# Six modulation jobs moved from attention to stand behind feed-forward units

## What is computed

```python
def ada_params(cond, w, b):
    m = (jax.nn.silu(cond) @ w + b)[..., None, :]
    return jnp.split(m, N_MOD, axis=-1)           # 9 vectors of 1024, per layer

def ffn_half(x, mods, g, w_gu, w_d):
    shift, scale, gate = mods
    h = modulate(rmsnorm(x, g), shift, scale) @ w_gu
    hg, hu = jnp.split(h, 2, axis=-1)
    return x + 0.5 * gate * ((jax.nn.silu(hg) * hu) @ w_d)

ml = ada_params(c, mod_w[l], mod_b[l])            # latent tokens
mc = ada_params(c_ctx, mod_w[l], mod_b[l])        # context tokens
xl = ffn_half(xl, ml[0:3], ...)                   # f0 (layer 0), f2 (layer 1)
hl = modulate(rmsnorm(xl, mix_norm[l]), ml[3], ml[4])
xl = xl + ml[5] * mixer(hl)
xl = ffn_half(xl, ml[6:9], ...)                   # f1 (layer 0), f3 (layer 1)
```

## Time and profile before

| what | us |
|---|---|
| median of three runs | 1909.67 |
| lowest, highest | 1908.73, 1921.3 |
| profiled execution, first to last instruction (span) | 1913.4 |
| of it PE busy | 1820.4 |
| DVE busy | 850.8 |
| ACT busy | 626.8 |
| jobs' products on PE (L510, 1024 records) | 69.3 |

### The profile page before, as it was taken

The page is one execution under the profiler, slowest core; times in us unless marked ns, Lnnn a source line. Parts: engine busy times, 40 slices in busy tenths (PEclk is TensorE's granted clock), DMA queues, the critical chain, the costliest instruction groups (busy, mean ns, idle before and its releaser), DMA issues.

```text
span 1913.4 us, 25250 instructions
## 1 busy us (share of the span) xinstructions
PE 1820.4 (95%) x10210; PEld 1503.0 (79%) x10210; DVE 850.8 (44%) x1269; ACT 626.8 (33%) x839; POOL 34.2 (2%) x68
## 2 busy tenths in 40 slices
PE   6899999999878899999999999999999999899997
PEld 4688888877544578888888788888886998899996
DVE  4333233345868453333233533333344446765454
ACT  3322122233464333222222432222224323544342
POOL 0000000000001000000000000000000000000000
PEclk8899999999989899999999999999999999999998
DMA  8522543234119344222223432232123212355543
GB/s 325 222 107 72 186 183 108 70 118 181 46 47 388 159 155 176 104 83 101 108 72 102 157 110 99 83 106 109 63 94 153 89 67 94 109 197 182 190 160 105
DMA packets 39683, 252.40 MB, mean 132 GB/s; under 512 B 4528, under 2 KB 6064, under 8 KB 15152
## 3 DMA queue, kind: packets, MB, share of 16 engines
q1 hardware_dynamic: 30384, 184.10, 26.9%
q0 software_dynamic: 9216, 67.11, 8.9%
HBM read 250.15 MB, written 1.05 MB: 131 GB/s over the span
## 4 chain that ended last, share of the span: by engine, by line
PE 87%; DVE 7%; ACT 3%; DMA 2%; issue 1%; SPq 0%; ACTq 0%; DVEq 0%
PE ps L477 26%; PE ps L479 26%; PE ps L478 26%; PE ps L510 2%; DVE y L1506 2%; DVE w_lo L1312 1%; ACT w_hi L995 1%; PE ps L863 1%; DMA mod_raw<-in_mod_w 1%; PE ps L892 1%; DVE t_ring L1368 1%; DVE hn_lo L1375 1%; PE ps L739 0%; DVE gact L1550 0%; PE ps L889 0%
## 5 line engine op out<-in xcount | busy, mean ns | idle before, releaser
L477 PE MATMUL ps<-hn_hi,w_hi 128*128 128x512 f32 (+2 forms) x1784 | 648.5, 364 | 22.5 <-DVE hn_lo L1375 15.7
L479 PE MATMUL ps<-hn_hi,w_lo 128*128 128x512 f32 (+2 forms) x1784 | 640.3, 359 | 0.0
L478 PE MATMUL ps<-hn_lo,w_hi 128*128 128x512 f32 (+2 forms) x1784 | 640.2, 359 | 0.0
L1312 DVE TENSOR_TENSOR w_lo<-raw,w_hi 128x2048 fp32r<-128x2048 f32 (+2 forms) x184 | 377.0, 2049 | 571.0 <-ACT w_hi L995 570.8
L995 ACT ACTIVATE w_hi<-raw 128x2048 fp32r<-128x2048 f32 (+2 forms) x184 | 316.5, 1720 | 747.2 <-PE ps L479 739.8
L477 PEld LDWEIGHTS ps<-hn_hi,w_hi 128*128 128x128 f32 (+1 forms) x1784 | 338.6, 190 | 86.1 <-DVE hn_lo L1375 19.5
L479 PEld LDWEIGHTS ps<-hn_hi,w_lo 128*128 128x128 f32 (+1 forms) x1784 | 338.6, 190 | 50.6 <-issue 0.8
L478 PEld LDWEIGHTS ps<-hn_lo,w_hi 128*128 128x128 f32 (+1 forms) x1784 | 338.6, 190 | 47.8 <-issue 0.5
L477 PE MATMUL ps<-a_hi,w_hi 128*128 128x512 f32 (+1 forms) x704 | 255.6, 363 | 1.7 <-DVE a_lo L1437 1.7
L478 PE MATMUL ps<-a_lo,w_hi 128*128 128x512 f32 (+1 forms) x704 | 255.2, 363 | 0.0
L479 PE MATMUL ps<-a_hi,w_lo 128*128 128x512 f32 (+1 forms) x704 | 255.2, 362 | 0.0
(11 more groups left out here) (202 smaller groups left out, 1134.9 us busy)
## 6 DMA issues: line engine op xcount, KB each, us to landing
raw<-in_w_up SPq DMA_DIRECT2D x88, 1024.0 KB, 4.8
mod_raw<-in_mod_w POOLq DMA_DIRECT2D x64, 1024.0 KB, 7.8
raw<-in_w_downA SPq DMA_DIRECT2D x32, 768.0 KB, 4.3
raw<-in_w_downB SPq DMA_DIRECT2D x32, 640.0 KB, 3.9
raw<-in_w_od_in SPq DMA_DIRECT2D x16, 1024.0 KB, 4.8
mod_raw<-in_mod_first SPq DMA_DIRECT2D x8, 1024.0 KB, 7.6
raw<-in_w_ev_in SPq DMA_DIRECT2D x7, 1024.0 KB, 4.8
raw<-in_w_ev_out SPq DMA_DIRECT2D x4, 1024.0 KB, 4.9
```

The lines of the kernel that those rows point to most:

```text
L477: pe.matmul(o, lh, rh, start=first, stop=False)
L478: pe.matmul(o, lh, rl, start=False, stop=False)
L479: return pe.matmul(o, ll, rh, start=False, stop=last)
L1312: dve.tensor_tensor(w_lo[:, u0 % 2, 0:n], raw[:, u0 % 2, 0:n], w_hi[:, u0 % 2, 0:n], ALU.subtract).then_inc(lo_made, 1)
```

## The change

Jobs 6 to 11 leave attention, and `ATT_JOBS`, `ATT_FROM`, `att_quarters` and `att_rows` go with them, as do two waits of PE (`unit_evac` ahead of job 6's products, `mod_made` for job 11 ahead of `ev_out`). `UP_JOB` now gives each part of f0 and f1 a tuple of jobs, one for each pair from the first on: the products stand behind unit 0 of the pair, the columns behind unit 1. Job 3 leaves the down units of f0A. Norms 1 and 2 carry jobs 8 and 9 instead of 5 and 12. `pairs` runs as many pairs outside the loop as its `first` says: on PE in f0A four instead of one, and in f0B, f1A and f1B two instead of one each. Banks of the former attention jobs become 4 and 5. `mix_out` gets a wait for its vector.

```diff
-        UP_JOB = {"f0A": 2, "f0B": 4, "f1A": 13}
-        DOWN_JOB = {"f0A": 3}
-        NORM_JOB = {1: 5, 2: 12, 3: 14, 4: 15, 5: 17}
-        ATT_JOBS = range(6, 12)
+        UP_JOB = {"f0A": (2, 3, 4, 5), "f0B": (6, 7), "f1A": (10, 11), "f1B": (12, 13)}
+        NORM_JOB = {1: 8, 2: 9, 3: 14, 4: 15, 5: 17}
         KEY_JOB = 16
-        ATT_FROM = 10
...
-        def pairs(eng, n, body, first=False):
-
-            lo = 1 if first else 0
-            if first:
-                body(0, False)
+        def pairs(eng, n, body, first=0):
+
+            lo = int(first)
+            for r in range(lo):
+                body(r, False)
...
                         first = isinstance(r, int) and r == 0
+                        up_job = up_jobs[r] if isinstance(r, int) and r < len(up_jobs) else None
...
-                            if first and up_job and j == 0:
+                            if up_job and j == 0:
                                 mod_products(up_job, 0, 4)
-                            if first and up_job and j == 1:
+                            if up_job and j == 1:
                                 mod_columns(up_job)
 
-                    pairs(pe, nf // 2, pair, True)
+                    pairs(pe, nf // 2, pair, max(1, len(up_jobs)))
...
-                            if first and down_job and j == 0:
-                                mod_products(down_job, 0, 4)
-                            if first and down_job and j == 1:
-                                mod_columns(down_job)
...
-                between += [(mod_products, (m, q, q + 1)) for m, q in att_quarters(j)]
                 if j + 1 < NJ:
                     score(j + 1, 0)
-                    if ATT[j + 1][1] == 1:
+                    if ATT[j + 1][1] == 1 and between:
...
-                for m in att_rows(j):
-                    mod_columns(m)
...
-            pe.wait_ge(mod_made, vector_done(ATT_JOBS[-1]))
...
-                for m in att_rows(j):
-                    mod_rows(m)
...
-                for m in att_rows(j - 1):
-                    mod_vector(m)
...
             def mix_out(name, n, w):
+                dve.wait_ge(mod_made, vector_done(3 * n - 1))
```

More of the change, by code:

```diff
@@ L262, in build @@
         GAIN = [("ffn1", 0), ("mix", 0), ("ffn2", 0), ("ffn1", KT), ("mix", KT), ("ffn2", KT), ("final", 0)]
-        UP_JOB = {"f0A": 2, "f0B": 4, "f1A": 13}
-        DOWN_JOB = {"f0A": 3}
-        NORM_JOB = {1: 5, 2: 12, 3: 14, 4: 15, 5: 17}
-        ATT_JOBS = range(6, 12)
+        UP_JOB = {"f0A": (2, 3, 4, 5), "f0B": (6, 7), "f1A": (10, 11), "f1B": (12, 13)}
+        NORM_JOB = {1: 8, 2: 9, 3: 14, 4: 15, 5: 17}
         KEY_JOB = 16
-        ATT_FROM = 10
         def product_bank(m):
-            return 2 if m in ATT_JOBS else 4
+            return 4
         def column_bank(m):
-            if m in ATT_JOBS:
-                return 3
             return bank(U["od_gate"], 1) if m in (KEY_JOB - 1, KEY_JOB) else 5
@@ L287, in block_place @@
             return mod_raw[:, 2 * q:2 * q + 2, :].rearrange("p a (b n) -> p (a b) n", n=LAT)
[L289 to L296, removed]
         CONV_AT = {0: ((2, 4), (2, 5)), 1: ((2, 6),), 2: ((2, 7),), 4: ((3, 0),), 5: ((3, 1), (3, 2)),
@@ L503, in mod_products @@
                     pe.wait_ge(mod_row, vector_done(m - 1))
-                if q0 == 0 and m == ATT_JOBS[0]:
-                    pe.wait_ge(unit_evac, U["ev_in"] + 7)
                 for q in range(q0, q1):
@@ L607, in ffn @@
                     up, down = U[f"{name}up{part}"], U[f"{name}down{part}"]
-                    up_job, down_job = UP_JOB.get(name + part), DOWN_JOB.get(name + part)
+                    up_jobs = UP_JOB.get(name + part, ())
                     def pair(r, end):
                         first = isinstance(r, int) and r == 0
+                        up_job = up_jobs[r] if isinstance(r, int) and r < len(up_jobs) else None
                         if first and part == "A":
@@ L1045, in ffn @@
                     up, down = U[f"{name}up{part}"], U[f"{name}down{part}"]
-                    up_job, down_job = UP_JOB.get(name + part), DOWN_JOB.get(name + part)
+                    up_jobs = UP_JOB.get(name + part, ())
                     a0 = ABASE[name] + tile
                     def pair(r, end):
-                        first = isinstance(r, int) and r == 0
+                        up_job = up_jobs[r] if isinstance(r, int) and r < len(up_jobs) else None
                         for j in range(2):
@@ L1059, in pair @@
                             act.activation(a_hi[:, j + 2 * r, 0:w], prod[:, j, 0:w], ACT.Copy).then_inc(a_hi_made, 1)
-                            if first and up_job and j == 0:
+                            if up_job and j == 0:
                                 mod_rows(up_job)
                     act.preload_act_table(ACT.Silu)
-                    pairs(act, nf // 2, pair, bool(up_job))
+                    pairs(act, nf // 2, pair, len(up_jobs))
                     tile += nf
@@ L1076, in down_pair @@
                                 square_tile(n + 1, j, r, w)
-                            if first and down_job and j == 0:
-                                mod_rows(down_job)
-                    pairs(act, KT // 2, down_pair, part == "B" or bool(down_job))
+                    pairs(act, KT // 2, down_pair, part == "B")
             act.wait_ge(c_loaded, 16)
@@ L1438, in pair @@
                                               ALU.subtract).then_inc(a_made, 1)
-                            if first and up_job and j == 1:
+                            if up_job and j == 1:
                                 mod_vector(up_job)
-                    pairs(dve, nf // 2, pair, a0 == 0 or bool(up_job))
+                    pairs(dve, nf // 2, pair, max(a0 == 0, len(up_jobs)))
                     if part == "A":
@@ L1459, in down_pair @@
                                 rest_of(down + j + 2 * r + 2)
-                            if first and down_job and j == 1:
-                                mod_vector(down_job)
-                    pairs(dve, KT // 2, down_pair, part == "B" or bool(down_job))
+                    pairs(dve, KT // 2, down_pair, part == "B")
             dve.memset(eps[:], EPS)
```

## The result

| | before | after |
|---|---|---|
| median of six runs, us | 1911.38 | 1918.65 |
| lowest to highest, us | 1906.73 to 1921.3 | 1918.06 to 1920.54 |
| profiled execution: its time, us | (none kept) | 1918.35 |
| its span, us | 1913.4 | 1916.6 |

The ratio after to before is 1.0043, with a 95% interval of 1.0023 to 1.0062: some 8 us slower, between 4 and 12, which is within 1%. The kernel before ran again beside the experiments, 73 executions in four groups with medians of 1908.63, 1909.75, 1908.62 and 1910.49 us; against those, 1918.65 us is 8 to 10 us more.

What follows compares the result with a forecast made beforehand. PE was taken as full in feed-forward units, attention as bound by DVE, then by weight transfers. Six jobs at 4.3 us (+25.8) less 17.2 in attention give +8.6 on 1909.67, so 1918.3 us; range 1910 to 1928.

Steps and rivals of the forecast that it cites:

- The sum: Whole kernel: +25.8 us in feed-forward units and -17.2 in attention make +8.6 us, 1918.3 us.
- Six jobs at 4.3 us: Feed-forward units f0 and f1: six more jobs on full PE, each paid at its whole length, +25.8 us.
- Nothing for transfers: Feed-forward units: refills of job weights cause no wait, 0 us, upper bound 2 us at each of two tight places.
- The tight place: Jobs 2 and 3 in f0: last refill lands by 89.5 us, its quarter is read at 92.0, margin 2 us.
- Rival 3: Feed-forward units: refills land late at two tight places of 2 us, +12.6 us, 1922.3 us; chance 0.04.
- Nothing for peeling: Feed-forward units: more straight code and less loop costs nothing, as both run gapless.
- The tail: End of attention: without jobs DVE sets the pace, layer-norm sums end 18.6 us earlier; net -17.2 us with the clock.
- The clock term: End of attention: PE's clock rises near 623 us, so the first `ev_out` matmuls run at half speed, +1.4 us.
- Rival 1: Attention: PE stays at 1.2 GHz until the normed tiles come, +15.7 us, 1925.4 us; chance 0.08.
- Rival 2: Attention: becomes a chain of latencies, DVE waits on scores five times 5.33 us, +35.6 us, 1945 us; chance 0.06.
- That the tail is a queue for transfers: Attention from 600 to 632 us: jobs queue for weights, eight 1 MB quarters wanted every few microseconds, 8.8 us through one transfer.

Runs made afterwards that it cites:

- e12: Changed kernel with half the row tiles of the products left out in the ten jobs behind feed-forward units, transfers whole: 1903.92 us, 0.9964 of before.
- e4: Kernel before, jobs where they were, with the same pairs outside the loops as in the changed kernel: 0.9999 of before.
- e1: Kernel before with the transfers that attention triggers (weights of jobs 7 to 12) cut to an eighth, all matmuls kept: 1893.59 us, 0.994 of before.
- e3: Changed kernel with 8 extra matmuls of constants on PE in each of attention steps 10 to 21, without transfers: 1932.57 us, 1.0137 of before.
- e2: Kernel before with 8 instead of 32 product matmuls in each of jobs 6 to 11 (three of four column groups out), transfers whole: 1.0009 of before.
- e11: Changed kernel with three of four column groups of products left out in the ten jobs behind feed-forward units, transfers whole: 1919.99 us, 1.0059 of before.
- e6: Changed kernel with four jobs (6 to 9) back in attention, 10 in norm 2, 11 to 13 in f1: 1905.44 us, 0.9978 of before.
- e8: Changed kernel with four jobs back in attention, job 13 in norm 3 and job 14 behind unit 0 of f2: 1902.79 us, 0.9965 of before.

## Why the prediction was right, point by point

- **The sum.** +8.6 us were forecast, 1918.3 us; measured 1918.65 us, and +8 us by the ratio. The stages that the change touches make +25.9 - 18.8 = +7.1 us. That the time itself came within 0.4 us is luck: the sum was added to 1909.67 us, the median of three executions, where six gave 1911.38 and the later groups 1908.6 to 1910.5.
- **Six jobs at 4.3 us.** +12.95 and +12.94 us in f0 and f1, 25.9 against 25.8. e12 shows that it is PE's own time, and with it that a job behind a unit costs no less than its length.
- **Nothing for transfers.** PE waits for `mod_raw` nowhere in the trace of after, and no engine waits for a load in f0 or f1 (66 to 440 and 680 to 1080 us). The tight place held: the first quarter of job 3 had been read at 89.72 us, the last at 92.31, where 92.0 was forecast for its start; the refills of job 3 landed within 14.8 us of their issue, the last by 87.8 us. Rival 3 falls.
- **Nothing for peeling.** e4, to within 2 us.
- **The tail.** -17.2 forecast, -18.8 in the two traces, -15.3 against e4's tail, with the range of -10.1 to -20.2 given. The taps ended 57.4 us behind the gate, where 56.3 were forecast (617.6 - 561.3): the one wait of DVE, 0.99 us for scores that PE made at a mean clock of 0.67 (602 to 607.2 us), was not foreseen. The sums ended 58.8 us behind it, 58.9 forecast, though by two errors that cancel (next point). The 18.6 us that the working gives for this step start from the one trace of before with the long tail; against e4's, 3.5 us of it were never there to be given back.
- **The clock term was mis-sized.** Forecast: the last two sums at 1.2 GHz (3.3 us) and 1.4 us more in the `ev_out` matmuls. Measured: the last four records took 1.98 us, at a granted clock of 1.00, and the 24 matmuls 5.5 us, as before. The values at 623.02 us and the first two sums at 624.92 us (3.78 us, at the low level) came just ahead, and by 629.88 us the clock had risen. I had counted work only from the third sum on. The 1.3 us that the sums took less cancel the 1.1 us by which the taps ended later; the 1.4 us in `ev_out` are what remains of the difference to -17.2. Rival 1, in which the clock stays low until the normed tiles, falls.
- **Rival 2, latencies in attention.** It had one wait of 0.99 us where 10.5 would have turned the case. The low clock did show (0.67 instead of 0.91) and, with DVE setting the pace, can have cost no more than that wait ahead of the taps' end. What it would be worth to lift it isn't shown: e3's filler did so and cost more than it could bring.
- **That the tail is a queue for transfers.** e1 carries it for most, 11.7 to 15.2 us, and leaves 3.6 to the jobs' matmuls and the small transfers. The reading behind it was loose: not eight such megabytes were wanted every few microseconds, but one each 2.5 us (the 22 issues from 578.63 to 631.11 us).

Half settled is how the 3.5 us by which the tail of before varies come about. The sums of e4, on PE's timeline:

```profile
632.10 3.68 PE L770 MATMUL ps<-y,mats 128*128 128x512 f32 x8
```

They started 70.3 us behind the gate and took 3.7 us, at a clock of 1.00 (632 to 636 us); before, by the same view, they started 70.9 us behind it and took 6.7, at 0.56 (632 to 639). That makes up the 3.5 us. From 608 to 614 us the clock was at 0.50 before and at 1.00 in e4, and DVE waited 4.80 and 2.14 us for the same head. What makes the clock differ between executions of the same program no run set or shows.

## What to carry to other kernels

A side job costs its whole length on an engine that is full, and next to nothing in the gaps of one that waits, up to what its transfers allow: here three of six jobs were free in attention, and moving all six gave up that half (-6 us against +8). Work that an engine does while another sets the pace is free, at a low clock too; the same engine's work at the end of the stretch, as the sums here, is paid for at its whole length and at whatever clock it then has. Before filling a gap, read the busy time of the engine over it, for the chain of waits may run elsewhere while the engine works. And where a filler waits for a transfer, look at what stands behind it in the queue: it is too early there if results are wanted soon, and too late if it leaves earlier gaps empty.

## What the hardware showed that I had not expected

- Product matmuls of 32 columns of weights, in the four column groups, run side by side: 64 records in 3.66 us, and 16 of one group alone in 3.64 us. The Trainium skill states it ("TensorE: Matmul & The Clock Gate", Part 3: Packing small matmuls — row/col tiling): small tiles at different positions of the array run concurrently. The traces agree, with the two times just given; so leaving three groups out, as e2 and e11 do, takes nothing from PE's time.
- PE's mean clock in attention stood at 0.66 for 57 us (573 to 630), and DVE lost 0.99 us at the most by it; it was back at 2.4 GHz before the `ev_out` matmuls.
- The same attention program met different clocks at the same place: 0.66 in e6 (608 to 613 us) and 1.00 in e8 (607 to 611), 0.50 before and 1.00 in e4 (608 to 614). The tails differed by 3.4 and 3.5 us.
